# Hybrid decoder trunk on 8 cores: half-size filler pieces, a longer skew, masks added in PSUM, an early gate tile and another block order

## The chip, the cores and the metric

The kernel runs on all 8 cores of one Trainium2 chip. Each core computes 2 of the 16 sequences from end to end, with its own copy of the weights; the cores exchange nothing. A time is the device time of the slowest core in microseconds. A run of the kernel before took 4423.77 us in the median of 3 runs (3996.86 to 4560.96).

## The reference

Two layers, each a token mixer and a feed-forward part, on x of shape (16, 2048, 1024):

```
h = rms_norm(x) * g_pre;  proj = h @ w_in            # q, k, v of 16 heads, 2 gate logits of width 1024
o_A: dilated sliding window attention, 3 groups of 4 heads, (window, dilation) = (128,1), (512,4), (2048,16),
     the groups combined by their softmax denominators
o_B: 4 heads, causal block-sparse: own block of 256 keys + the best 3 past blocks (gate = q . mean(k of block))
y = (sigmoid(g_A) * (o_A @ W_A) + sigmoid(g_B) * (o_B @ W_B)) @ w_out;   x = x + rms_norm(y) * g_post
u = gelu(causal_dwconv3(h2 @ W_gate)) * (h2 @ W_up);                     x = x + rms_norm(u @ W_down) * g
```

Both attentions subtract m_h * (t - s) from the scores, and a query sees no later key.

## The kernel before, in words

Everything is written as Python generators. Each `yield c` says "about c us of TensorE work have been issued". `merge(main, fill, ratio)` (L83) steps the main generator and, for each c that it yields, lets the filler issue until it has yielded c * ratio. So the order of instructions on every engine is fixed when the program is built, and TensorE takes its own in that order: one that waits holds up all behind it. `par` interleaves generators by their yielded sums.

One sequence and one layer ("a layer" below; a core does four) goes through these stages:

1. Six dilated units (`dil_unit`, L660), 16 steps each, one step a tile of 128 keys for two heads. A step issues two score matmuls (L681) into a pair of PSUM banks, an exp on ScalarE (L689), a multiplication by the mask and distance factors on VectorE (L694), and, SKEW = 2 steps later, the products with V (`pv_mm`, L656) of the earlier tile. The filler is the projection work of the next unit: `v_proj` (L606) and `proj_fm` (L621), which issues 8 matmuls of 128x512 as one piece (`mm_group`, L383) and yields 1.75. The last unit, (2, 1), has two key and query projections of the block-sparse heads as filler; their evacuation puts a copy on ScalarE, a copy and for keys a reduction (L805) on VectorE. Every fourth step two banks of V products are copied by ScalarE (L372) and added into the accumulators by GpSimd (L740).
2. The block-sparse stage (`moba`, L868). It walks over 8 blocks (query group qg of 512, head pair); a block has 4 * qg + 4 key tiles times two heads, 160 units in all. A unit issues one score matmul (L935), an exp (L943), for the four diagonal key tiles a multiplication by the triangle on VectorE (L947), and 4 units later the V product (L656). When a block ends, VectorE copies the two accumulators (L964) and frees their banks (two banks only, so the next block's first V product needs that), and a chain of small transfers and VectorE operations follows that turns the denominators into factors: store, gather, reciprocal (L900), store, broadcast, multiply (L892). The steps of the chain are issued a fixed number of units after the end of the block (`todo`).
3. The filler of that stage (`fill_m`), ratio 1.25: the last projection, the block selection (`gating`, L809) of both pairs, the denominators of dilated pair 1 (`dil_den`, whose VectorE multiplications are L777), then it waits until the four blocks of query groups 0 and 1 are done, then `gates` (L975) for the first half of the tokens: per output chunk and token tile two gate projections of 8 matmuls, two tanh (L993, L999), two branch products of 2 matmuls (L383), and three VectorE operations (L1005, L1011, L1014). Each token tile of `gates` issues one of the 8 loads of `wout_t` once the last key tile of block (3, 0) has been issued, because that tile lies over the pair 0 operands.
4. `gates` for the second half, with `tail_out(0)` (output projection, L538, norms, residual) as filler; the first tanh there waits for the end of the block-sparse chains. Then the feed-forward part, L383 and L1242, whose first half has `tail_out(1)` as filler. The normalised tiles reach `hT` through transposing DMAs on SyncE's queue (L175).

The weights come through a ring of 8 slabs on GpSimd's queue (L180); each release waits on GpSimd for TensorE.

## Time and profile before

| | us |
|---|---|
| median of 3 runs (lowest, highest) | 4423.77 (3996.86, 4560.96) |
| profiled execution, its own time | 3906.2 |
| span of its slowest core (all: 3892.4 to 3904.9) | 3904.9 |
| TensorE busy | 3765.8 (96%) |
| VectorE, ScalarE, GpSimd busy | 2078.2, 1762.5, 877.7 |
| mean granted TensorE clock, by core | 0.991 to 0.994 |

Busy time of TensorE counts the tail of each matmul, so the 96% are a little kind. The trace's times below are microseconds from the start of the span of core 3. The first dilated unit of the first layer starts at 80.6, its last one at 243.1, the block-sparse stage at 269.1, and the 73rd of its 160 units at 320.6.

### The profile page before, as it was taken

The numbers are of one execution on the slowest core, as the hardware profiler recorded it, in microseconds if no ns is written. First come the engines' busy times: TensorE is split into PE (matmuls) and PEld (weight loads), VectorE is DVE, ScalarE is ACT, GpSimd is POOL, SyncE is SP. The second block draws the span as 40 slices with busy tenths as digits, with TensorE's granted clock in tenths as the row PEclk, the third lists the DMA queues.
The fourth block names the chain that finished last, engine by engine and source line by source line (L and its number), as shares of the span: only waits on it lengthen the run. The fifth ranks groups of instructions, "written<-read, shape, count | busy, mean of one in ns | idle before, by whom it ended". The sixth has DMA issues, their size and how long they took to land.

```text
span 3904.9 us, 56082 instructions; the slowest of 8 cores (3892.4 to 3904.9 us)
## 1 busy us (share of the span) xinstructions
PE 3765.8 (96%) x19760; PEld 1810.6 (46%) x19760; DVE 2078.2 (53%) x3265; ACT 1762.5 (45%) x3541; POOL 877.7 (22%) x1484
## 2 busy tenths in 40 slices
PE   6989999999998999999999899999999989999999
PEld 4544444444553444444465344444446534444444
DVE  4454566464346466646434646654643554675463
ACT  3456345253345635535334653552533465354251
POOL 2331232111132133211113213321111322331110
PEclk9999999999999999999999999999999999999999
DMA  6133789454313489875632259994442225797341
GB/s 147 29 72 51 153 173 169 112 97 90 81 32 65 60 165 177 149 171 79 129 79 53 48 77 167 158 156 124 77 105 52 53 47 92 161 179 133 103 71 70
DMA packets 303867, 410.37 MB, mean 105 GB/s; under 512 B 150560, under 2 KB 167200, under 8 KB 303584
## 3 DMA queue, kind: packets, MB, share of 16 engines
q0 software_dynamic: 118656, 190.89, 33.3%
q1 hardware_dynamic: 184944, 215.88, 21.6%
q8 instruction: 171, 2.80, 0.3%
q14 instruction: 96, 0.79, 0.1%
HBM read 500.52 MB, written 67.63 MB: 145 GB/s over the span
## 4 chain that ended last, share of the span: by engine, by line
PE 91%; DVE 4%; ACT 2%; DMA 1%; issue 1%; POOL 0%; SPq 0%; ACTq 0%; POOLq 0%; DVEq 0%
PE psum L383 55%; PE psum L1242 16%; PE psum L538 5%; PE psum L606 5%; PE psum L656 5%; PE psum L935 3%; PE psum L681 2%; ACT s_arena L943 1%; DMA s_xr<-x 1%; DVE s_arena L777 1%; DVE s_arena L694 1%; DVE s_arena L375 1%; ACT s_tz L372 0%; SPq L175 0%; DVE s_hb L460 0%
## 5 line engine op out<-in xcount | busy, mean ns | idle before, releaser
L383 PE MATMUL psum<-s_hT,s_slabs 128*128 128x512 bf16 x9728 | 2180.4, 380 | 12.3 <-DVE s_arena L1203 9.2
L383 PEld LDWEIGHTS psum<-s_hT,s_slabs 128*128 128x128 bf16 x9728 | 940.2, 98 | 1115.7 <-issue 32.1
L1242 PE MATMUL psum<-s_arena 128*128 128x512 bf16 x2816 | 609.1, 379 | 0.0
L1192 DVE SCALAR_TENSOR_TENSOR s_arena<-s_arena,s_convw 128x512 f32<-128x512 f32 x352 | 264.3, 751 | 425.9 <-ACT s_arena L1184 425.8
L1242 PEld LDWEIGHTS psum<-s_arena 128*128 128x128 bf16 x2816 | 275.6, 98 | 332.2
L656 PE MATMUL psum<-s_arena 128*128 128x128 bf16 (+2 forms) x1840 | 354.3, 268 | 63.7 <-DVE s_arena L947 21.5
L420 DVE SCALAR_TENSOR_TENSOR s_tz<-psum,s_stat,s_gpost 128x1024 f32<-128x1024 f32 x128 | 164.1, 1282 | 381.1 <-POOL s_stat L399 381.1
L411 ACT ACTIVATE s_hb<-psum 128x1024 bf16<-128x1024 f32 x128 | 131.0, 1023 | 502.2 <-PE psum L1242 344.0
L943 ACT ACTIVATE s_arena<-psum 128x512 bf16<-128x512 f32 (+3 forms) x640 | 296.1, 547 | 72.5 <-PE psum L935 61.1
L180 POOL DMA_DIRECT2D s_slabs<-w_in_r x224 | 122.5, 550 | 905.8 <-PE psum L656 453.6
L694 DVE TENSOR_TENSOR s_arena<-s_arena,s_dmask 128x512 bf16<-128x512 bf16 (+1 forms) x384 | 192.0, 504 | 217.9 <-ACT s_arena L689 216.2
L1183 ACT COPY s_arena<-psum 128x512 f32<-128x512 f32 x352 | 205.1, 583 | 203.7 <-PE psum L383 203.7
L396 POOL TENSOR_SCALAR s_stat<-s_stat 128x1 f32<-128x1 f32 x256 | 61.6, 241 | 1028.1 <-ACT s_hb L411 574.6
L689 ACT ACTIVATE s_arena<-psum 128x512 bf16<-128x512 f32 (+1 forms) x384 | 190.5, 504 | 200.0 <-PE psum L681 200.0
L1184 ACT ACTIVATE s_arena<-psum,s_convw 128x512 f32<-128x512 f32 x352 | 276.0, 784 | 0.0
L451 ACT ACTIVATE s_hb<-s_xr 128x1024 bf16<-128x1024 f32 x128 | 135.2, 1056 | 301.7 <-DVE s_xr L426 249.0
L1195 DVE SCALAR_TENSOR_TENSOR s_arena<-s_arena,s_convw 128x512 f32<-128x512 f32 x352 | 264.7, 752 | 12.5
L180 POOL DMA_DIRECT2D s_slabs<-w_gate_r x176 | 97.5, 554 | 749.6 <-PE psum L383 747.7
L460 DVE SCALAR_TENSOR_TENSOR s_hb<-s_xr,s_stat,s_gpre 128x1024 bf16<-128x1024 f32 x128 | 164.3, 1284 | 175.9 <-POOL s_stat L399 167.6
L606 PE MATMUL psum<-s_slabs,s_hT 128*128 128x256 bf16 x2048 | 250.1, 275 | 5.1 <-DVE s_arena L375 5.1
L1203 DVE TENSOR_TENSOR s_arena<-s_arena,psum 128x512 bf16<-128x512 f32 x352 | 239.5, 680 | 3.6 <-ACT s_arena L1201 3.6
L935 PE MATMUL psum<-s_arena 128*128 128x512 bf16 (+3 forms) x640 | 225.2, 361 | 8.5 <-ACT s_arena L943 5.7
(71 smaller groups left out, 3278.9 us busy)
## 6 DMA issues: line engine op xcount, KB each, us to landing
s_slabs<-w_in_r POOLq DMA_DIRECT2D x224, 256.0 KB, 4.8
xs<-s_xr SPq DMA_DIRECT2D x96, 512.0 KB, 3.9
s_xr<-xs SPq DMA_DIRECT2D x96, 512.0 KB, 5.2
s_slabs<-w_gate_r POOLq DMA_DIRECT2D x176, 256.0 KB, 4.6
s_slabs<-w_up_r POOLq DMA_DIRECT2D x176, 256.0 KB, 5.7
s_xr<-x SPq DMA_DIRECT2D x64, 512.0 KB, 6.4
s_arena<-w_down POOLq DMA_DIRECT2D x88, 256.0 KB, 7.3
y<-s_xr SPq DMA_DIRECT2D x32, 512.0 KB, 2.9
```

The costliest lines, as they stand in the source:

```text
L180: q.eng.dma_start(out=out, in_=in_, **kw).then_inc(so.sem, 16)
L383: inst = nc.tensor.matmul(out, lhsT=l_, rhs=r_, start=(i == 0), stop=(i == n - 1))
L606: inst = nc.tensor.matmul(ps[b][:, 0:256], lhsT=hT[:, kc, start:start + 127 * d + 1:d], rhs=rhs, start=(kc == 0), stop=(kc == 7))
L656: return nc.tensor.matmul(out, lhsT=V[:, tile, VOFF[hd]:VOFF[hd] + 128], rhs=rhs, start=start, stop=stop)
L694: ptoks[kt] = DVE.do(nc.vector.tensor_tensor(out=Pd[sl][:, :, 0:nq], in0=Pd[sl][:, :, 0:nq], in1=dmask[:, head:head + 2, 0:nq], op=ALU.mult))
L935: tS = PE.do(nc.tensor.matmul(ps[bS][:, 0:nq], lhsT=Kx[:, kt * 128:(kt + 1) * 128], rhs=Qx[:, qg * 512 + c0:(qg + 1) * 512], start=True, s ...
L943: tE = ACT.do(nc.scalar.activation(out=Pm[sl][:, 0:nq], in_=ps[bS][:, 0:nq], func=AF.Exp))
L1184: tt1 = ACT.do(nc.scalar.activation(out=t1_, in_=ps[b_a], func=AF.Identity, bias=convw[:, l, fc, 3:4], scale=convw[:, l, fc, 2:3]))
L1192: d1 = DVE.do(nc.vector.scalar_tensor_tensor(out=t1_, in0=a_[:, 1 + 512 * tgi:513 + 512 * tgi], scalar=convw[:, l, fc, 1:2], in1=t1_, op0= ...
L1195: d2 = DVE.do(nc.vector.scalar_tensor_tensor(out=t1_, in0=a_[:, 512 * tgi:512 + 512 * tgi], scalar=convw[:, l, fc, 0:1], in1=t1_, op0=ALU. ...
L1203: u1 = DVE.do(nc.vector.tensor_tensor(out=uT[:, u["fc"], u["tsl"]], in0=u["t1"], in1=ps[u["b_u"]], op=ALU.mult))
L1242: inst = nc.tensor.matmul(ps[zb + n], lhsT=uT[:, kc, i * 128:(i + 1) * 128], rhs=wdn[kc][:, n * 512:(n + 1) * 512], start=(kc == 0), stop= ...
```

## The change

- `merge` takes any number of fillers, each with its own ratio. `scaled` multiplies what a generator yields, `pause` yields without issuing.
- `proj_fm` and the gate projections yield after 4 of 8 matmuls (0.87) and after the other 4 (0.87).
- The skew in `dil_unit` is 3, not 2.
- In `moba`, the diagonal tiles of query groups 0 and 1 get their mask from a second matmul, identity times `ntri` (128 columns), accumulated on the scores before the exp; the VectorE multiplication remains for groups 2 and 3. The exp waits for the last dilated V product (`p_free`) and no longer for GpSimd's accumulation.
- The blocks run (2,0), (3,0), (2,1), (3,1), before (2,0), (2,1), (3,0), (3,1).
- In the norm chain of the first four blocks the gather is issued after 5 units (6), the reciprocal after 11 (16), the multiplication after 17 (16).
- The filler of the block-sparse stage becomes two fillers of ratio 1.25: `side` (selection of both pairs, the second after a pause of 8, and the denominators) and `fill_pe` (the last projection stretched by 1.5, then `gates`). `gates` issues the gate projections and tanh of output chunk 0 early, stretched by 3.4, into buffers of their own (`AB0`), then waits for `ready()`, then continues.

```diff
@@ def proj_fm
-                tp = mm_group(ps[b], [(buf[:, kc * 128:(kc + 1) * 128], hT[:, kc, tg * 512:(tg + 1) * 512]) for kc in range(8)],
-                              [tokw, hT_tok[4 * tg:4 * tg + 4]])
+                for kc in range(8):
+                    inst = nc.tensor.matmul(ps[b], lhsT=buf[:, kc * 128:(kc + 1) * 128], rhs=hT[:, kc, tg * 512:(tg + 1) * 512],
+                                            start=(kc == 0), stop=(kc == 7))
+                    if kc == 3:
+                        yield 0.87
+                tp = PE.do(inst)
                 bank_free[b] = consume(tg, b, tp)
-                yield 1.75
+                yield 0.87
@@ def dil_unit
-            SKEW = 2
+            SKEW = 3
@@ def moba
-            blocks = [(0, 0), (1, 0), (0, 1), (1, 1), (2, 0), (2, 1), (3, 0), (3, 1)]
+            blocks = [(0, 0), (1, 0), (0, 1), (1, 1), (2, 0), (3, 0), (2, 1), (3, 1)]
-                todo.append([16 if k < 4 else 28, lambda: norm_mult(k, qg, pair, rt)])
+                todo.append([17 if k < 4 else 28, lambda: norm_mult(k, qg, pair, rt)])
-                todo.append([6 if k < 4 else 10, gather])
-                todo.append([16 if k < 4 else 24, lambda: norm_recip(k, qg, pair, tl)])
+                todo.append([5 if k < 4 else 10, gather])
+                todo.append([11 if k < 4 else 24, lambda: norm_recip(k, qg, pair, tl)])
+                    diag = kt >= 4 * qg
+                    pe_mask = diag and qg < 2
+                    inst = nc.tensor.matmul(ps[bS][:, 0:nq], lhsT=Kx[:, kt * 128:(kt + 1) * 128],
+                                            rhs=Qx[:, qg * 512 + c0:(qg + 1) * 512], start=True, stop=not pe_mask)
+                    if pe_mask:
+                        inst = nc.tensor.matmul(ps[bS][:, 0:128], lhsT=identb[:, :], rhs=ntri[:, :], start=False, stop=True)
-                    ACT.wait(tS, pfree[sl], waits)
+                    ACT.wait(tS, pfree[sl], p_free)
-                    if kt >= 4 * qg:
+                    if diag and not pe_mask:
@@ def gates (each token tile: gate_mm = 2 x 8 matmuls and tanh, branch_mm = 2 x 2 matmuls and the VectorE part)
+            if early is not None:
+                bufs, e_wait, factor, ready = early
+                for tgi in range(2):
+                    yield from scaled(gate_mm(0, tgi, bufs, e_wait), factor)
+                while not ready():
+                    yield 0.5
+                for tgi in range(2):
+                    yield from branch_mm(0, tgi, bufs)
+                first = 1
@@ def mixer
-            def fill_m():
-                yield from par(chain(mqk_proj(l, 1, 0, w1, mq[1], FB2), gating(1, mq[1], aug_t[1], sel[1], FB2)),
-                               gating(0, mq[0], aug_t[0], sel[0], FB2), dil_den(1, m_wait, nt1))
-                while not all((q, p) in done for q in range(2) for p in range(2)):
-                    yield 0.5
-                yield from gates(l, 0, nt1, ob_done, FB2, nt1, mts, wout_load)
-            merge(moba(mq, aug_t, sel, vt[3], done, m_wait, on_p0), fill_m(), 1.25)
+            def ready():
+                return len(nt1) == 4 and all((q, p) in done for q in range(2) for p in range(2))
+            def fill_pe():
+                yield from scaled(mqk_proj(l, 1, 0, w1, mq[1], FB2), 1.5)
+                yield from gates(l, 0, nt1, ob_done, FB2, nt1, mts, wout_load, (AB0, nt0, 3.4, ready))
+            side = par(chain(pause(8.0), gating(1, mq[1], aug_t[1], sel[1], FB2)),
+                       gating(0, mq[0], aug_t[0], sel[0], FB2), dil_den(1, m_wait, nt1))
+            merge(moba(mq, aug_t, sel, vt[3], done, ures[(2, 1)]["pv_tok"], m_wait, on_p0), (side, 1.25), (fill_pe(), 1.25))
```

## Rows read from the trace of the kernel before

**Rows 1.** The page: busy time of the engines; chain that ended last, by engine.
```profile
PE 3765.8 (96%) x19760; PEld 1810.6 (46%) x19760; DVE 2078.2 (53%) x3265; ACT 1762.5 (45%) x3541; POOL 877.7 (22%) x1484
...
PE 91%; DVE 4%; ACT 2%; DMA 1%; issue 1%; POOL 0%; SPq 0%; ACTq 0%; POOLq 0%; DVEq 0%
```
**Rows 2.** Windows: stretch, length, busy by engine (x count), clock, DMA share, GB/s.
```profile
80.60:117.40 36.80, 36.48 (x288) 24.05 (x288) 14.66 (x32) 15.67 (x31) 3.95 (x6) 1.00 0.34 49
...
211.40:243.10 31.70, 29.23 (x187) 13.16 (x186) 19.90 (x33) 15.80 (x32) 13.23 (x13) 1.00 0.49 86
243.10:269.10 26.00, 20.43 (x128) 8.93 (x126) 15.85 (x28) 13.09 (x33) 13.32 (x10) 1.00 0.32 59
...
305.60:320.60 15.00, 13.02 (x49) 4.86 (x48) 6.83 (x20) 11.38 (x24) 0.00 (x0) 0.77 0.12 37
...
512.00:704.00 192.00, 191.90 (x889) 86.72 (x888) 127.41 (x165) 104.10 (x217) 52.48 (x106) 1.00 0.88 169
```
**Rows 3.** Chain that ended last, one feed-forward piece: start, us, what.
```profile
609.45 94.97 PE psum L383 x440
```
**Rows 4.** Timeline of TensorE in the last dilated unit: start, us, what [idle before].
```profile
258.04 0.22 PE L656 MATMUL psum<-s_arena 128*128 128x128 bf16 x1 [1.07 <-DVE s_km L805]
...
258.48 1.89 PE L383 MATMUL psum<-s_hT,s_slabs 128*128 128x512 bf16 x8
...
264.47 0.22 PE L656 MATMUL psum<-s_arena 128*128 128x128 bf16 x1 [1.07 <-DVE s_km L805]
...
268.59 0.27 PE L656 MATMUL psum<-s_arena 128*128 128x128 bf16 x2 [1.31 <-DVE s_arena L694]
```
**Rows 5.** Timeline of VectorE there.
```profile
257.19 0.69 DVE L805 TENSOR_REDUCE s_km<-psum 128x2 f32<-128x512 f32 x1
...
257.80 0.28 DVE L694 TENSOR_TENSOR s_arena<-s_arena,s_dmask 128x256 bf16<-128x256 bf16 x1
```
**Rows 6.** TensorE by shape, 269.1 to 320.6: busy us, mean ns, idle before.
```profile
L935 PE MATMUL psum<-s_arena 128*128 128x512 bf16 x42 | 17.2, 427 | 0.6 <-ACT s_arena L943 0.3 <-issue 0.3
L656 PE MATMUL psum<-s_arena 128*128 128x512 bf16 x42 | 16.8, 403 | 4.2 <-DVE s_arena L947 1.4 <-DVE s_gsm L840 1.1 <-DVE s_cdm L900 1.0
L383 PE MATMUL psum<-s_hT,s_slabs 128*128 128x512 bf16 x32 | 7.6, 379 | 0.7 <-ACT s_tz L372 0.7
...
L858 PE MATMUL psum<-s_identb,s_gsel 128*8 128x128 bf16 x32 | 2.4, 219 | 0.0
```
**Rows 7.** Waits of TensorE, 269.1 to 320.6: us in total, times, longest.
```profile
PE psum L656 <- DVE s_arena L947: 5.5, 5, 1.4
PE psum L935 <- ACT s_arena L943: 1.3, 2, 0.9
PE psum L656 <- DVE s_gsm L840: 1.1, 2, 0.8
```
**Rows 8.** ScalarE's exp and VectorE's mask, 269.1 to 320.6.
```profile
L943 ACT ACTIVATE s_arena<-psum 128x512 bf16<-128x512 f32 (+3 forms) x72 | 31.7, 524 | 13.4 <-PE psum L935 10.6 <-POOL s_xr L740 2.7
...
L947 DVE TENSOR_TENSOR s_arena<-s_arena,s_tri 128x128 bf16<-128x128 bf16 x39 | 7.8, 220 | 13.8 <-ACT s_arena L943 13.4
```
**Rows 9.** Timeline, end of the block-sparse stage: TensorE, SyncE's queue, VectorE, ScalarE.
```profile
400.54 0.22 PE L656 MATMUL psum<-s_arena 128*128 128x128 bf16 x1
...
413.21 0.35 SPq L180 DMA_DIRECT2D dm<-s_cdm  x1
418.71 1.08 SPq L180 DMA_DIRECT2D s_arena<-dm  x2
...
428.95 1.40 DVE L892 TENSOR_TENSOR s_arena<-s_arena 64x512 bf16<-64x512 f32 x2
...
430.38 0.60 ACT L993 ACTIVATE s_arena<-psum 128x512 f32<-128x512 f32 x1 [3.19 <-DVE s_arena L892]
```
**Rows 10.** Timeline, feed-forward start of the third layer: SyncE's queue, TensorE.
```profile
2504.19 12.19 SPq L175 DMA_TRANSPOSE s_hT<-s_hb  x1
...
2547.67 2.72 PE L383 MATMUL psum<-s_hT,s_slabs 128*128 128x512 bf16 x6 [8.91 <-DVE s_arena L1203]
```

More of the change, by code:

```diff
@@ L80, with merge, scaled, pause @@
 KB = 256
-def merge(main, fill, ratio):
-    credit = 0.0
-    live = fill is not None
+def merge(main, *fills):
+    live = [[gen, ratio, 0.0] for gen, ratio in fills]
     for cost in main:
-        credit += cost * ratio
-        while live and credit > 0:
-            try:
-                credit -= next(fill)
-            except StopIteration:
-                live = False
-    if live:
-        for _ in fill:
-            pass
+        for f in list(live):
+            f[2] += cost * f[1]
+            while f[2] > 0:
+                try:
+                    f[2] -= next(f[0])
+                except StopIteration:
+                    live.remove(f)
+                    break
+    for f in live:
+        for _ in f[0]:
+            pass
+def scaled(gen, factor):
+    for cost in gen:
+        yield cost * factor
+def pause(cost):
+    for _ in range(int(2 * cost)):
+        yield 0.5
 def chain(*gens):
@@ L572, in build @@
         AB = [carve((12 + 2 * i) * KB, 512) for i in range(4)]
+        AB0 = [carve((60 + 2 * i) * KB, 512) for i in range(4)]
         uT = carve(0, 11264, BF16).rearrange("p (c t) -> p c t", c=NFC)
@@ new lines, in gates, with gate_mm @@
+            w = {}
+            def gate_mm(oc, tgi, bufs, waits):
+                tg = 2 * hf + tgi
+                tsl = slice(tg * 512, (tg + 1) * 512)
+                if tgi == 0:
+                    w[oc] = [load_w(l, 24 + oc), load_w(l, 32 + oc)]
+                out = []
+                for j in range(2):
+                    buf, tok, s_ = w[oc][j]
+                    b = banks.get()
+                    PE.wait(tok, hT_tok[4 * tg:4 * tg + 4])
+                    inst = None
+                    for kc in range(8):
+                        inst = nc.tensor.matmul(ps[b], lhsT=buf[:, kc * 128:(kc + 1) * 128], rhs=hT[:, kc, tsl], start=(kc == 0), stop=(kc == 7))
+                        if kc == 3:
+                            yield 0.87
+                    t_g = PE.do(inst)
+                    ACT.wait(t_g, abf[2 * tgi + j], waits)
+                    s1 = ACT.do(nc.scalar.activation(out=bufs[2 * tgi + j], in_=ps[b], func=AF.Tanh, scale=0.5))
+                    bank_free[b] = [s1]
+                    out.append(s1)
+                    if tgi == 1:
+                        slab_ring.release(s_, t_g)
+                    yield 0.87
+                w[(oc, tgi)] = out
@@ L1286, in qk_tg @@
                     next(gen)
+                    next(gen)
                 yield
```

93 lines of the change are left out of this document (41 added, 52 removed).

## The prediction

> **What bounds the kernel now.** I read the page first: TensorE is busy for 96% of the span and the chain of work that ended last lies on it for 91% [rows 1]. So only what shortens TensorE's own queue, or the holes in it, can move the end. The windows by stage show where the holes are: the feed-forward stretch has 0.1 us of idle time in 192, the first dilated unit 0.3 in 36.8, but the fifth unit 2.5 in 31.7, the last one 5.6 in 26.0, and the first 72 units of the block-sparse stage have long waits and, in their last 15 us, a granted clock of 0.77 [rows 2]. The rest of the layer is paid in matmuls at full rate: 440 of 128x512 in 94.97 us, 0.216 us each [rows 3]. I use that as the price of 512 columns, and a quarter of it, 0.054, for 128.
>
> How much is to be had: in the block-sparse stretch from 269.1 to 320.6 (51.5 us) TensorE has 42 + 42 + 32 matmuls of 512 columns, 25.1 us, and the smaller shapes and the selection come to some 8.7 us more by their columns: 33.8 us of work, so 17.7 us are lost [rows 6]. Waits for another engine explain some 10, of which the group of waits has the three largest [rows 7]. The slow clock explains about 3.5: 15.0 us at 0.77 are 6.9 us at 1.2 GHz, half of it lost [rows 2]. The rest is scores and V products short of exps. With the 8.1 us of the two last dilated units that makes about 26 us a layer, 103 in all, 2.6%: hardly more is to be had here.
>
> The sum is made against the profiled execution, 3906.2 us (span 3904.9). The median of the runs shown is 4423.77, 13% above it, and none of the three came down to it (lowest 3996.86). I carry the saving over as a ratio.
>
> **The last dilated unit.** Once in four steps (6.4 us) the V product waits 1.07 us, put down to VectorE's key reduction, and the filler of 8 matmuls, 1.89 us, comes only behind it [rows 4]. VectorE began the reduction at 257.19 for 0.69 us and the mask product at 257.80 [rows 5]: the product that TensorE needed stood behind it. Skew 3 puts one step more between the exp and the V product, 0.22 us of matmuls and, with pieces of half size, 0.87 us of filler in every step instead of 1.73 in every second. That is 1.1 us more, about one such wait. I take 3.7 of the unit's 5.6 us away; bounds 1.5 (where the wait just moves to the copies that free the V banks, 0.3 us each four steps) and 5. At the end of each unit the V product of tile 15 waits for its mask, 1.31 us at the last one [rows 4]; one more V product of 0.2 us stands before it, so 0.2 a unit, 1.2 for six, bounds 0 and 2. The fifth unit's idle time I leave, but for that. Sum 4.9, rounded down to 4.5 because splitting pieces also lets the bank of a projection be held longer.
>
> **The masks in PSUM.** 32 diagonal units a layer lose their VectorE product (0.22 us and a semaphore hop [rows 8]) and gain a matmul of 128 columns. 5.5 us of TensorE waits ended with that product, 5 times [rows 7]; only the one in block (2, 0) keeps it. I take away 4.4. The price is 32 x 0.054 = 1.7 us, above it 32 x 0.075 = 2.4 by the busy time of the 32 selection transposes of 128 columns, 2.4 us [rows 6]. I take 1.7, as these stand between other matmuls.
> For the same price the Trainium skill ("TensorE: Matmul & The Clock Gate", Back-to-back issue gap) states about 81 ns for each weight load and matmul of 128 columns in a stream; by it the masks would cost 2.6 us a layer, 10.4 in all, where I have 7, and the saving would be 46 us. No row here shows 81; the transposes, tails included, have 75.
>
> **The exp's wait.** The first exp stood 2.7 us behind GpSimd's accumulation [rows 8]; it now goes when the last V product is done. TensorE had 1.3 us of waits for exps and most of its 0.7 us at the first filler piece in that place [rows 6, 7]; I take 1.5 us.
>
> **The early gate tile.** Four groups of 8, 32 x 0.216 = 6.9 us of TensorE work, are issued between units 20 and 63 (10.4 of stretched projection, then 7 x 3.4 = 23.8, at 0.54 a unit). Moved work saves nothing by itself; it saves what it puts into holes. ScalarE has 31.7 us of exps in 51.5 us [rows 8], plus 4 tanh of 0.6: it doesn't bind. The holes left there after the two edits above are 17.7 - 4.4 - 1.5 = 11.8 us, 3.5 of it slow clock. With fewer and shorter stops I expect the clock to stay up (3) and one more microsecond filled. What is late next: the V banks behind VectorE's copies at each block's end, and these behind the selection's operations (1.1 us [rows 7]) and the denominator products. So about 7.8 remain. Check: 33.8 + 1.7 + 6.9 + 7.8 = 50.2 us to the 73rd unit instead of 51.5, with 6.9 us of gate work done: 8.2 us a layer. Bounds: 4 (only the mask and exp waits go, and the clock doesn't rise) and 13.
>
> **What costs nothing.** One constant load of 32 KB at the start. The earlier reciprocal can stop VectorE for its gather, but with no mask behind it no exp product waits. `ready()` is true at about unit 78, before 82: the same gates earlier, hidden in a stretch already full. The order of the blocks moves 8 loads of the output weights 24 units forward; they land long before the first output tile, before as after.
>
> **The end of the stage.** The filler is used up earlier. Gates take 70.4 of yields at 0.54 a unit, before from unit 83 to 214; now 63.4 from 78 to 196, so TensorE gets about 16 us of filler behind the last V product instead of the 26.7 seen from 400.54 [rows 9]. The chain of the last block: reciprocal's store at +12.7, its landing 5.5 us later, broadcast, multiplication at +28.4, only then the first tanh, which had waited 3.19 us [rows 9]. The multiplication comes behind the last filler piece on VectorE and so moves up to about +24. Behind the filler TensorE has four gate groups, two branch pairs and one output tile, 6.9 + 1.7 + 3.5 = 12 us, that need no tanh: cover to +28. So no hole, but thin cover: 0.3 us as cost, bounds 0 and 4.
>
> **Sum.** 4.5 + 8.2 - 0.3 = 12.4 us a layer, 50 in four: 3856 us for the profiled execution, 1.3% less. On the median that is 4423.77 x 0.987 = 4367.
>
> **Rivals.**
> *More (chance 0.12).* All early stops go, and the 15 us at a clock of 0.77, which came after mask waits of up to 1.4 us [rows 2, 7], with them. Then 13 + 7 = 20 us a layer, 80 us, 3826 (median 4333), over 2% faster. Against it: TensorE takes its queue in order, and the V bank waits are untouched.
> *Less (0.22).* The holes are latencies in series (score, exp, product, V bank) and the filler stands in front of the waits without shortening them; masks cost 1.7. Then 1.5 + 3 = 4.5 a layer, 18 us, 3888 (4404). For it: TensorE was idle although filler of 7 us lay in the first 13 units.
> *The change does not get to its place (0.06)*: half pieces and skew 3 cancel out (the third step without scores at each unit's end is not covered): 0 +- 8 us, 3906.
> *Slower (0.06).* The transposing DMAs ahead of the feed-forward part. In the third layer one occupied SyncE's queue for 12.19 us and TensorE stood 8.91 us with the clock down after it [rows 10], 13 us in all against the other layers. Earlier weights could bring such a pile-up to every layer and to both tails: 2 x 13 x 4 = 104 against 50 gained, 3960 (4485), 1.4% slower. It decides from 6 us of stall a tail. Against it: DMA share is 0.88 there already [rows 2] without a stall, and the output weights leave that place earlier.
>
> **Numbers.** A measurement of this kernel tells 2% from no change. My forecast has 0.54; over 2% faster 0.12, within 2% 0.84 (forecast, less, no effect and the milder part of slower), over 2% slower 0.04 (stalls half as long again). In the profiled execution's terms 8 in 10 lie between 3830 and 3915. The runs shown spread by 14%, far more than any case here, and the time after is one of that kind; so the range goes from the low end of the first, 3835, to the highest run shown with little gained, 4560.96 x 0.998 = 4550.
>
> **What would show it.** Right: the last dilated unit at 21 to 23.5 us for 26.0; no mask wait of TensorE in the first 48 block-sparse units; the 73rd unit at about 50 us from the first, with 32 gate matmuls before it, no stretch there under 0.9 of clock; gaps behind the last block under 1 us; feed-forward windows unchanged. Wrong: the same waits with VectorE's copies as releaser, or a first tanh of the second half behind L892 for over 8 us with TensorE idle.

## The result and the profile after

The changed kernel takes 3859.1 us, the median of its runs, and the kernel before some 3904 us beside it: a ratio of 0.989, 95% interval 0.986 to 0.992. The change makes it faster by 1.1%, more than the comparison is uncertain and less than 2%. In some runs of either kernel the cores of one die are slowed and the time is up to 18% longer; all the runs of before that the prediction was shown (3996.86 to 4560.96) were of this kind, while the profiled execution of 3906.2 us and the times compared below are not. The profiled execution after took 3857.86 us, 48.3 us less than the one before; its slowest core took 3856.3 us from first to last instruction.

The page after, lines as in [rows 1], and the group of V products:

```profile
span 3856.3 us, 56276 instructions; the slowest of 8 cores (3849.7 to 3856.3 us)
...
PE 3763.9 (98%) x19888; PEld 1816.3 (47%) x19888; DVE 2062.1 (53%) x3137; ACT 1773.1 (46%) x3541; POOL 876.4 (23%) x1484
...
PE 93%; DVE 3%; ACT 2%; issue 1%; DMA 0%; POOL 0%; SPq 0%; ACTq 0%; DVEq 0%; POOLq 0%
...
L676 PE MATMUL psum<-s_arena 128*128 128x128 bf16 (+2 forms) x1840 | 351.9, 265 | 27.1 <-DVE s_kmb L840 9.0
```

TensorE is busy for as long as before, 3763.9 us for 3765.8, though it has 128 matmuls more; only its idle time shrank, from 139 us to 92. The windows after, in the order of [rows 2] (first, fifth and sixth dilated unit, the first block of the block-sparse stage, its next three, the fifth up to the 73rd unit, a feed-forward stretch):

```profile
83.30:119.80 36.50, 36.45 (x286) 23.97 (x286) 14.55 (x32) 15.57 (x31) 3.87 (x6) 1.00 0.33 50
215.00:245.20 30.20, 29.37 (x185) 12.94 (x184) 20.31 (x32) 15.77 (x31) 11.34 (x12) 1.00 0.48 88
245.20:270.00 24.80, 21.34 (x131) 8.73 (x129) 19.83 (x31) 13.60 (x34) 14.48 (x12) 0.99 0.32 65
270.00:279.70 9.70, 9.16 (x52) 4.22 (x53) 1.05 (x3) 4.58 (x11) 3.01 (x2) 0.67 0.21 30
279.70:308.90 29.20, 27.57 (x193) 14.29 (x192) 19.52 (x65) 20.12 (x45) 0.57 (x1) 1.00 0.29 66
308.90:321.50 12.60, 12.44 (x59) 4.77 (x56) 5.84 (x16) 11.79 (x27) 3.17 (x6) 1.00 0.55 85
500.00:692.00 192.00, 191.89 (x889) 86.70 (x888) 129.02 (x167) 102.64 (x211) 53.34 (x109) 1.00 0.88 165
```

The last dilated unit still has 3.5 us without work for TensorE (before 5.6). On this core and in this layer the slow clock that lay in the last 15 us up to the 73rd unit is gone from there and stands at the beginning of the stage. Over all cores and layers there is less of it: the time at the lower clock is 57.8 us a core before and 36.7 after. Ahead of the first dilated unit and in the rest of the layers it hardly changed (together 24.5 and 22.2 us), but in the last dilated unit and the block-sparse stage it fell from 33.3 to 14.5 us, from 8.3 to 3.6 us a layer. At half the speed, half of such time is lost, so this gives back 2.4 us a layer. The feed-forward part is what it was.

One core of one execution is a thin base for terms of a microsecond. For the comparisons below every trace is split at the first score matmul of each dilated unit, of the block-sparse stage and of its 73rd unit, and at the stage's last score. The columns are means over the four layers; "rest" goes from the last block-sparse score to the next layer's first dilated score, "layer" from one layer's first dilated score to the next layer's, both as the mean of the first three layers. Cores whose trace lacks records of block-sparse scores are left out of all columns but those two, which leaves six (three in the lines marked *):

```
us                        dilated units 1 to 6           sum    first 72  stage   rest   layer
before                    36.9 37.0 27.5 29.7 31.4 26.7  189.2  51.5      130.0   640.5  959.5
changed kernel            36.7 36.6 28.4 30.6 30.4 24.9  187.5  50.1      128.6   633.0  948.6
 skew 2                   36.9 37.0 27.5 29.4 30.0 23.6  184.4  49.9      128.7   633.3  946.1
 skew 4                   36.5 36.3 28.7 29.8 29.3 23.2  183.9  49.3      127.8   632.9  944.4
 whole filler pieces      36.7 36.6 27.9 30.2 31.0 26.4  188.7  51.6      133.1   632.5  953.8
 accumulation left out    36.7 36.3 28.2 30.6 30.4 22.6  184.7  48.6      127.1   633.0  944.6
 accumulation on VectorE  36.7 39.8 32.6 30.7 35.5 27.6  202.8  50.5      129.0   632.9  964.1
 skew 2, four-piece add * 36.9 36.5 26.9 29.4 29.7 25.8  185.2  49.6      128.1   632.8  945.8
 masks on VectorE         as the changed kernel          187.5  51.9      130.4   632.7  949.9
 no early gate tile       as the changed kernel          187.6  47.6      125.5   640.3  952.9
 exp's wait as before     as the changed kernel          187.6  50.7      129.2   633.0  949.5
 old order of the blocks  as the changed kernel          187.5  50.2      128.8   633.2  949.0
before, with skew 3 *     36.7 36.6 28.2 29.8 31.1 23.6  186.0  52.1      130.6   640.3  957.0
```

By this table the change takes 1.7 us off the dilated part, 1.4 off the block-sparse stage and 7.5 off the rest, and 10.9 us off a layer from start to start, 44 in four. The third layer's transposing DMAs, which cost the profiled core of before 13 us [rows 10], have no long one after, and TensorE waits there for 3.0 us:

```profile
2508.39 51.92 PE L396 MATMUL psum<-s_hT,s_slabs 128*128 128x512 bf16 x232 [2.97 <-DVE s_arena L1250]
```

That layer's rest is 5.6 us longer than the mean of the two before it, on this core as on the others; before, it was 12.5 us longer on the profiled core and 3.6 to 5.3 on the other seven. So the profiled core of before carried some 7 us that the others did not, and the pair of profiled executions flatters the change by that much. The change did not remove the stall of a typical core.

In the block-sparse stage the waits on masks are gone. TensorE's waits from 270.0 to 321.5 after, beside [rows 7], and its groups there, beside [rows 6]:

```profile
PE psum L676 <- DVE s_arena L989: 0.6, 1, 0.6
PE psum L643 <- ACT s_tz L385: 0.5, 1, 0.5
PE psum L676 <- DVE s_gsm L860: 0.5, 1, 0.5
PE psum L957 <- ACT s_arena L968: 0.3, 1, 0.3
```
```profile
L1017 PE MATMUL psum<-s_hT,s_slabs 128*128 128x512 bf16 x32 | 8.2, 379 | 0.0
L960 PE MATMUL psum<-s_ntri,s_identb 128*128 128x128 bf16 x32 | 7.5, 233 | 0.0
```

The 32 mask matmuls and the 32 gate matmuls are where the prediction placed them. Over the complete cores and all layers TensorE has 2.2 us without work between the stage's start and the 73rd unit; before it had 9.9. At the end of the stage stands one wait of 1.0 us, before the first output tile. The multiplication came at 425.98, some 24 us behind the last V product (402.1), as the prediction had it:

```profile
421.83 3.61 PE L551 MATMUL psum<-s_arena 128*128 128x512 bf16 x16 [1.01 <-DVE s_arena L1048]
...
425.98 1.40 DVE L912 TENSOR_TENSOR s_arena<-s_arena 64x512 bf16<-64x512 f32 x2 [4.41 <-DMA s_arena<-dm]
```

What is left at the seam between the dilated part and the block-sparse stage is this. TensorE, VectorE and GpSimd at the end of the last dilated unit, changed kernel:

```profile
266.73 0.66 PE L676 MATMUL psum<-s_arena 128*128 128x128 bf16 x5 [0.15 <-ACT s_tz L385]
269.56 0.37 PE L676 MATMUL psum<-s_arena 128*128 128x128 bf16 x2 [2.17 <-DVE s_kmb L840]
...
267.15 0.69 DVE L825 TENSOR_REDUCE s_km<-psum 128x2 f32<-128x512 f32 x1 [0.17 <-ACT s_arena L385]
267.76 1.65 DVE L714 TENSOR_TENSOR s_arena<-s_arena,s_dmask 128x256 bf16<-128x256 bf16 x1
269.33 0.16 DVE L840 TENSOR_SCALAR s_kmb<-s_km 128x8 bf16<-128x8 f32 x1
...
266.24 3.02 POOL L760 TENSOR_TENSOR s_xr<-s_xr,s_tz 128x512 f32<-128x512 f32 x2 [2.34 <-ACT s_tz L385]
```

The V product of the last tile needs the mask product that began at 267.76. Such a product takes 0.28 us elsewhere [rows 5]; here it took 1.65 and ended at 269.41, just behind GpSimd's two additions (269.26). The wait is put down to L840 only because that was VectorE's last instruction. Behind the 2.17 us of idle time the granted clock falls here: the first 52 matmuls of the stage took 9.7 us at a mean of 0.67. Between the levels of 2.4 and 1.2 GHz that is two thirds of the stretch at the lower one. In the second layer the clock stayed up, and 52 matmuls took 6.2 us:

```profile
1220.00:1226.20 6.20, 6.20 (x52) 3.42 (x53) 1.05 (x3) 4.48 (x11) 3.02 (x2) 1.00 0.36 48
```

The wait is there in every layer, 2.2 to 2.3 us, so it does not decide alone. In the 24 seams of the six complete cores the clock fell around the stage's first score in 22; with skew 2 and a wait of 1.38 us in 19, with the accumulation left out and 0.8 to 0.9 us in 2. Yet before, with 1.31 us there and 1.08 us four microseconds earlier, it fell in 8 only. What else decides stays open.

### The profile page after: what moved, and what is told of

Read it like the earlier page. It is cut to its first block, busy times and chain, and to the rows that moved or that the text cites. A ratio compares the mean times of both kernels' runs of the same rounds, so it can differ in the third digit from the quotient of the medians.

```text
span 3856.3 us, 56276 instructions; the slowest of 8 cores (3849.7 to 3856.3 us)
## 1 busy us (share of the span) xinstructions
PE 3763.9 (98%) x19888; PEld 1816.3 (47%) x19888; DVE 2062.1 (53%) x3137; ACT 1773.1 (46%) x3541; POOL 876.4 (23%) x1484
## 4 chain that ended last, share of the span: by engine, by line
PE 93%; DVE 3%; ACT 2%; issue 1%; DMA 0%; POOL 0%; SPq 0%; ACTq 0%; DVEq 0%; POOLq 0%
PE psum L396 34%; PE psum L1289 16%; PE psum L1017 11%; PE psum L643 11%; PE psum L551 6%; PE psum L676 5%; PE psum L620 5%; PE psum L957 3%; PE psum L701 2%; ACT s_tz L385 1%; DVE s_arena L714 1%; DVE s_hb L473 0%; DMA s_xr<-x 0%; ACT s_arena L385 0%; ACT s_hb L464 0%
## 5 line engine op out<-in xcount | busy, mean ns | idle before, releaser
L396 PE MATMUL psum<-s_hT,s_slabs 128*128 128x512 bf16 x5632 | 1224.0, 379 | 3.0 <-DVE s_arena L1250 3.0
L643 PE MATMUL psum<-s_hT,s_slabs 128*128 128x512 bf16 x2048 | 497.7, 382 | 4.8 <-DVE s_arena L389 3.1
L1017 PE MATMUL psum<-s_hT,s_slabs 128*128 128x512 bf16 x2048 | 489.6, 379 | 0.4
L968 ACT ACTIVATE s_arena<-psum 128x512 bf16<-128x512 f32 (+3 forms) x640 | 306.0, 539 | 90.8 <-PE psum L957 63.5
L1242 DVE SCALAR_TENSOR_TENSOR s_arena<-s_arena,s_convw 128x512 f32<-128x512 f32 x352 | 264.7, 752 | 12.5
```

Source lines behind the costliest of these rows:

```text
L396: inst = nc.tensor.matmul(out, lhsT=l_, rhs=r_, start=(i == 0), stop=(i == n - 1))
L643: inst = nc.tensor.matmul(ps[b], lhsT=buf[:, kc * 128:(kc + 1) * 128], rhs=hT[:, kc, tg * 512:(tg + 1) * 512], start=(kc == 0), stop=(kc = ...
L968: tE = ACT.do(nc.scalar.activation(out=Pm[sl][:, 0:nq], in_=ps[bS][:, 0:nq], func=AF.Exp))
L1017: inst = nc.tensor.matmul(ps[b], lhsT=buf[:, kc * 128:(kc + 1) * 128], rhs=hT[:, kc, tsl], start=(kc == 0), stop=(kc == 7))
L1242: d2 = DVE.do(nc.vector.scalar_tensor_tensor(out=t1_, in0=a_[:, 512 * tgi:512 + 512 * tgi], scalar=convw[:, l, fc, 0:1], in1=t1_, op0=ALU. ...
```

## Experiments

The first four ask what the dilated part lost, since 1.7 us a layer are there instead of 4.5.

**Skew 2 in the changed kernel.**
```
-            SKEW = 3
+            SKEW = 2
```


> The changed kernel with the skew of the dilated units back at 2; all else as changed. Lengths are counted from the first score matmul of a unit to that of the next. Changed kernel: last unit 24.8 to 25.0 us, all six units 187.5 in the mean of four layers; before: 26.2 (28.1 once) and 189.3. Theory of the prediction (the V product waits behind VectorE, and one more step covers it): the last unit goes back to 26 or more, all six to 189.5. Rival (what holds the V product is longer than a step, so the skew hardly matters, and only the half pieces gave the 1.3 us): last unit 25.2 or less, all six within 1 us of 187.5.

Measured: 3848.1 us (3843.9 and 3852.3), ratio to before 0.985 (0.980 to 0.990), 11 us less than the changed kernel. The longer skew, which the prediction counted as the gain, is a loss beside half pieces: the sum of the units falls from 187.5 to 184.4 when it is taken back. Neither the theory nor the rival had that.

**Whole filler pieces in the changed kernel.** The groups of eight matmuls, in the projections and in the gate tiles, are again issued without a yield in between (the cut of `proj_fm`; that of the gate projections is the same):
```
-                    if kc == 3:
-                        yield 0.87
-                yield 0.87
+                yield 1.74
```


> The changed kernel with filler pieces of 8 matmuls again, in the projections and the gate tiles. The third and fourth unit had become longer with the change (27.5 to 28.4 and 29.7 to 30.6 us), with a gap of 0.33 us every four steps at the V product that needs a bank back from ScalarE's copy. Theory A (half pieces leave only 0.87 us of filler before each such V product, where a whole piece covered the copy): third and fourth unit return to 27.4 and 29.8, the last unit rises to about 26. Theory B (the skew does it): both stay at 28.4 and 30.6. Block-sparse stage: first 72 units up by 1 to 3 us from 50 if half pieces matter there, unchanged if not.

Measured: 3879.2 us (3877.0 to 3879.9), ratio 0.993 (0.991 to 0.995). Taken out of the changed kernel, half pieces are worth 20 us, 5.2 us a layer, and most of it not where the prediction had looked: 1.2 us in the dilated units, 4.5 in the block-sparse stage, of which 1.5 up to the 73rd unit and 3.0 behind it. Those 3.0 are not a gain on the kernel before, which with its whole pieces takes 78.5 us from the 73rd unit to the last score, as the changed kernel does: whole pieces cost there only together with the other edits.

**The accumulation all but left out.** GpSimd's addition of the partial V sums runs over one column of 512, so that part of the sum is missing:
```
-    te = POOL.do(nc.gpsimd.tensor_tensor(out=dst, in0=dst, in1=src, op=ALU.add))
+    te = POOL.do(nc.gpsimd.tensor_tensor(out=U[:, m:m + 1], in0=U[:, m:m + 1],
+                                         in1=ust[k][:, 0:1], op=ALU.add))
```


> The changed kernel with GpSimd's accumulation of the dilated groups 2 and 3 cut to one column (the addition is left out; ScalarE's copies remain). In the trace mask products of VectorE that overlap one of GpSimd's additions take 1.0 us in the median and up to 3.14, the others 0.29 (128x256). Theory L (VectorE's product with two inputs in SBUF is held until GpSimd's addition ends, and that holds the V product): all mask products at 0.29 or 0.43, last unit 24.9 to 21.5, stall of 2.2 us before the block-sparse stage under 1 and no half clock after it, all six units 187.5 to 182. Theory B (the banks that ScalarE's copies free are the limit): mask products shorter, but the last unit stays above 24.3 and the 0.33 us gaps remain.

Measured: 3842.2 us, 17 less than the changed kernel. VectorE and TensorE at the same place:

```profile
268.74 0.28 DVE L714 TENSOR_TENSOR s_arena<-s_arena,s_dmask 128x256 bf16<-128x256 bf16 x1
...
269.17 0.27 PE L676 MATMUL psum<-s_arena 128*128 128x128 bf16 x2 [0.80 <-DVE s_kmb L840]
```

The product is back at 0.28 us and the wait at 0.80. Over the whole trace of the changed kernel the 100 products of 128x256 that met no addition had a median of 0.29 us, the 68 that met one 1.00, up to 3.14. With the short additions all of that is gone, the last unit falls from 24.9 to 22.6 us and the first 72 block-sparse units by 1.5. So GpSimd's additions, which no step of the prediction priced, cost 4 us a layer. The time at the lower clock falls with them from 36.7 to 24.2 us a core; half of the difference, 1.6 us a layer, is part of the 4. That VectorE is the way is shown by its products; what the additions cost otherwise, as by GpSimd's own queue, was not separated.

**The accumulation on VectorE**, straight from PSUM, without ScalarE's copy:
```
-    tc_ = copy_on(ACT, ust[k], ps[ub])
-    te = POOL.do(nc.gpsimd.tensor_tensor(out=dst, in0=dst, in1=src, op=ALU.add))
+    te = DVE.do(nc.vector.tensor_tensor(out=dst, in0=dst, in1=ps[ub], op=ALU.add))
+    bank_free[ub] = [te]
```


> The changed kernel with the accumulation moved: VectorE adds straight from PSUM into the accumulator, ScalarE's copy and GpSimd's addition are gone (same results). VectorE gets 8 operations of about 0.68 us a unit in four of six units, ScalarE loses 8 of 0.59, GpSimd 8 of 1.55. Theory L (hold behind GpSimd): as with the addition left out, less what VectorE's own time costs: last unit 22 to 23 us, all six 183 to 185, with the clock 4 x 6 = 24 us less than the changed kernel, ratio to before 0.982. Rival (VectorE becomes the bound: in the last unit 15.9 + 5.4 of 24.9 us busy, and the masks queue behind the additions): last unit 25 to 27, no gain, 0.989 or worse.

Measured: 3927.5 us, 68 more than the changed kernel, worse than even the rival expected. What takes the hold away puts the V banks behind VectorE's queue. TensorE's waits, whole trace:

```profile
PE psum L676 <- DVE s_xr L755: 39.0, 48, 1.4
...
PE psum L676 <- DVE s_arena L755: 27.4, 38, 1.0
```

Next, what skew 3 loses to skew 2. A theory by the phase of the filler, that is, by which steps of a unit have filler in front of their V product: when the V product that opens a new pair of banks falls into a step with little filler, ScalarE's two copies of the banks (1.07 us) or VectorE's products show.

**Skew 4 in the changed kernel**, run twice:
```
-            SKEW = 3
+            SKEW = 4
```


> The changed kernel with skew 4. With skew 3 the third to fifth unit have steps with one and with two half pieces in turn, and the V product that fills a bank falls in a step with one; with skew 2 it fell in one with two. Theory P (parity: ScalarE's two copies of 1.07 us are hidden only behind two half pieces): skew 4 behaves as skew 2 there, fourth unit 29.4 us (skew 3: 30.6), third 27.1 to 28.0 (28.1 to 28.7). Rival (a longer skew costs by itself, since a unit starts with that many steps without V products and ends with as many without scores or filler): fourth unit 31 or more, third 29. Last unit by both: no shorter than with skew 3 by more than 1 us, as the hold behind GpSimd stays.

> The changed kernel with SKEW = 4 in the dilated units instead of 3, the version I would keep, timed again because its first profile had a stretched die. My theory (with skew 3 the V product that opens a new bank falls into a step that has a single half piece of filler; with 2 or 4 into a step with two) expects 3838 to 3846 us, below the changed kernel by 13 to 21, fourth unit 29.8 and last unit 23.3 us in every undisturbed core. The rival, that each step of skew only costs the length of one more empty step at a unit's end, expects more than 3859, about 3862.

Measured: the first time four runs took 4010.0 to 4527.7 us, and only the spans of cores 4 to 7 of the profiled one compare, 3833.7 to 3837.6 us; the second time 3845.0 us median (three runs at 3843.6 to 3846.0, one at 3860.0), ratio to before 0.986 (0.983 to 0.989). Not more skew costs, but 3: fourth unit 29.7 us before, 30.6 with 3, 29.8 with 4, 29.4 with 2. The wait at the end of the last unit is another now:

```profile
266.11 0.22 PE L676 MATMUL psum<-s_arena 128*128 128x128 bf16 x1 [1.24 <-DVE s_km L825]
...
265.86 0.28 DVE L714 TENSOR_TENSOR s_arena<-s_arena,s_dmask 128x256 bf16<-128x256 bf16 x1
266.06 1.50 DVE L840 TENSOR_SCALAR s_kmb<-s_km 128x8 bf16<-128x8 f32 x1
...
266.00 3.02 POOL L760 TENSOR_TENSOR s_xr<-s_xr,s_tz 128x512 f32<-128x512 f32 x2 [2.48 <-ACT s_tz L385]
```

The mask product slipped in ahead of the additions, and the one held is a small key operation that TensorE does not need at once. Skew 4 and skew 2 are equal within their runs, and either beats both kernels. The third unit goes against the theory: it takes 28.7 us with skew 4, as long as with 3 (28.4) and not as with 2 (27.5).

**Skew 3 alone on the kernel before**, with its whole pieces:
```
-            SKEW = 2
+            SKEW = 3
```


> The kernel before with SKEW = 3 alone, whole filler pieces kept. The prediction held that skew takes the wait of 1.07 us that returned every four steps of the last unit; as the pieces stand behind the V product in every second step, it would be worth 1.5 to 3 us a layer: 3890 to 3896, last unit 24 to 25 us for 26.5. By the parity theory a gain at the last unit is paid back at units 3 to 5, where the bank-filling V product changes from the step with a filler piece to the one without: 3900 to 3912, fourth unit over 30.2 us for 29.7.

Measured: 3892.0 us for the lowest run, 10 to 14 less than before (3901.5 to 3905.9 beside it), 2.5 us a layer by the table, the last unit at 23.6 us for 26.7. The prediction's value for this unit, 3.7 us, holds about here (3.1), and my rule of payback at units 3 to 5, which asked for a fourth unit over 30.2 us, does not (29.8). What differs is seen when this trace is laid beside the one with whole pieces in the changed kernel: both have skew 3 and whole pieces in the last unit. The unit takes 25.4 us there and 22.4 here at full clock, 27.0 and 23.9 where the clock falls within it, so three microseconds either way. The last unit, in the changed kernel with whole pieces (first and second layer) and in the kernel before with skew 3 (second layer of one core, first layer of another):

```profile
243.80:269.20 25.40, 20.70 (x130) 9.15 (x130) 16.48 (x29) 13.18 (x33) 11.99 (x9) 1.00 0.32 64
1197.50:1224.50 27.00, 22.33 (x131) 9.39 (x128) 15.92 (x29) 13.11 (x33) 11.90 (x9) 0.94 0.30 59
```
```profile
1201.70:1225.60 23.90, 21.65 (x131) 9.20 (x129) 16.92 (x28) 13.12 (x33) 13.23 (x10) 0.93 0.34 67
242.20:264.60 22.40, 20.13 (x131) 8.96 (x129) 17.35 (x28) 13.16 (x33) 13.27 (x10) 1.00 0.38 72
```

TensorE's waits in the last unit, first the changed kernel with whole pieces (first layer; the second has the same), then the kernel before with skew 3 (second layer):

```profile
PE psum L674 <- DVE s_km L823: 2.2, 2, 1.1
PE psum L674 <- ACT s_tz L385: 1.5, 3, 1.2
PE psum L674 <- DVE s_arena L712: 0.8, 1, 0.8
```
```profile
PE psum L656 <- DVE s_arena L694: 2.1, 2, 1.4
```

And the place of the filler around the V product that opens new banks, in the same order:

```profile
252.57 0.28 PE L674 MATMUL psum<-s_arena 128*128 128x128 bf16 x2
252.78 0.23 PE L699 MATMUL psum<-s_arena 64*128 64x128 bf16 x2
254.18 0.50 PE L674 MATMUL psum<-s_arena 128*128 128x128 bf16 x2 [1.16 <-ACT s_tz L385]
254.59 1.89 PE L643 MATMUL psum<-s_hT,s_slabs 128*128 128x512 bf16 x8
```
```profile
1215.16 0.23 PE L681 MATMUL psum<-s_arena 64*128 64x128 bf16 x2
1215.32 0.28 PE L656 MATMUL psum<-s_arena 128*128 128x128 bf16 x2
1215.45 1.89 PE L383 MATMUL psum<-s_hT,s_slabs 128*128 128x512 bf16 x8
1217.27 0.23 PE L681 MATMUL psum<-s_arena 64*128 64x128 bf16 x2
1217.43 0.29 PE L656 MATMUL psum<-s_arena 128*128 128x128 bf16 x2
```

Counted from the unit's first score, the opening products are those of the steps 3, 7, 11 and 15. In the first kernel such a step (252.78) follows the V product before it at once, its piece comes only behind its own V product (254.59), and TensorE stands for 1.16 us; the next two such steps stand for 1.07 and 1.08. In the second a piece of 1.89 us lies ahead of each such step (1217.27), and no wait is left until the end of the unit. The kernel before has waits of the first kind, 1.07 us each [rows 4]. One more step of skew removed them there. Half pieces leave no step bare, and beside skew 3 they removed the waits of 1.07 to 1.16 us (in the changed kernel those places wait 0.16); then the second of the two has nothing to remove. That the place of the filler is the cause is read from two traces of kernels that differ in more than it; half pieces alone in the kernel before were not run.

**GpSimd's addition in four pieces**, with skew 2:
```
-    te = POOL.do(nc.gpsimd.tensor_tensor(out=dst, in0=dst, in1=src, op=ALU.add))
+    for p_ in range(4):    # a_, b_: a quarter of the columns of dst and src each
+        te = POOL.do(nc.gpsimd.tensor_tensor(out=a_, in0=a_, in1=b_, op=ALU.add))
```


> The changed kernel with skew 2 and GpSimd's accumulation in four instructions of 128 columns for each one of 512. With skew 2 alone: 3848 us, last unit 23.6 us, stall of 1.5 us at its end, mask products in its shadow up to 1.65 us. Theory L (a mask product is held until GpSimd's running instruction ends): the hold is at most one short instruction, 0.4 to 0.5 us; last unit 22 to 22.8, end stall about 1, 2 to 3 us a layer with the clock, so 3836 to 3842. Rival (GpSimd's next piece gets in again before VectorE, or its fixed cost makes the four much longer than one): mask products stay at 1 us or more, accumulation over 2.5 us a tile instead of 1.55, last unit 23.6 or longer, 3848 or more.

Measured: 3852.8 us the lowest run, profiled execution 3875.7 us, last unit 25.8 us for 23.6: no gain over skew 2, as the rival had it. Eight short additions back to back held one product 3.43 us, about as long as two long ones can (3.14 in the changed kernel):

```profile
243.86 3.43 DVE L714 TENSOR_TENSOR s_arena<-s_arena,s_dmask 128x256 bf16<-128x256 bf16 x1 [0.45 <-ACT s_arena L709]
...
243.34 3.81 POOL L765 TENSOR_TENSOR s_xr<-s_xr,s_tz 128x128 f32<-128x128 f32 x8
```

The last four take block-sparse edits one by one out of the changed kernel. The shifted steps of the norm chain, the stretching of the projection and the split of the filler in two were not taken out alone.

**Masks on VectorE again.**
```
-                    pe_mask = diag and qg < 2
+                    pe_mask = False
```


> The changed kernel with the masks of all diagonal tiles on VectorE again (no mask matmul). Theory of the prediction: the masks in PSUM take away 4.4 us of waits a layer for 1.7 of matmuls, so the first 72 block-sparse units get 2.7 us longer (changed kernel: 51.4, 48.0, 49.6, 51.2 us, of which up to 3.4 is slow clock), 11 us in all, 3869. Rival (the half pieces and the early gate tile cover those waits anyway): the stretch gets 1 to 2 us shorter by the matmuls left out, 3850 to 3854 in all.

Measured: 3867.3 us, 8 more; the first 72 units take 51.9 us instead of 50.1, and a layer 1.3 us more. So the masks in PSUM are worth 1.3 to 2 us a layer. TensorE waits there for the mask products 1.3 us a layer, where it waited 5.4 before the change, and for all engines 4.8 instead of 2.2: the expectations' rival is right in that the other edits had covered most of those waits, and wrong in that it expected a gain from leaving the masks out.

**No early gate tile.** The early argument is gone, and the gates begin, as before, when the blocks are done:
```
-    ... gates(..., wout_load, (AB0, nt0, 3.4, ready))
+    while not ready():
+        yield 0.5
+    ... gates(..., wout_load)
```


> The changed kernel without the early gate tile: the filler of TensorE waits for ready() after the projection and then does all of gates. Theory of the prediction: the tile's 6.9 us mostly go into holes, so that the first 72 units get only 3 to 4 us shorter without it and a layer 3 to 4 us longer, 12 to 16 us in all (3870 to 3874). Rival (the holes are waits in TensorE's own order, which the tile stands in front of): the 72 units get 6 to 7 us shorter and the whole stays within 4 us of 3858. A clock fall in the emptier stretch would add 1.7 us a time on top.

Measured: 3879.8 us, 21 more, 4.3 a layer by the table. The stage then takes 125.5 us instead of 128.6, and the rest of the layer 640.3 instead of 633.0: the tile's 6.9 us of work cost 3.1 where they were put and saved 7.3 where they had been. Two things pay for it. Up to the 73rd unit TensorE is without work for 5.3 us without the tile and 2.2 with it. And without it a core spends 12.8 us of its four layers at the lower clock between 15 us after the stage's start and the 73rd unit, with it none; half of that is 1.6 us a layer.

**The exp's wait as before**, for everything of the dilated part:
```
-    merge(moba(..., ures[(2, 1)]["pv_tok"], m_wait, on_p0), ...
+    merge(moba(..., m_wait, m_wait, on_p0), ...
```


> The changed kernel with the first exps of the block-sparse stage waiting as before, for everything of the dilated part and so for GpSimd's last addition, instead of the last V product. The prediction gave this wait 1.5 us a layer: 3865. If it is hidden because the scores of the first units wait for the matmuls and the slow clock anyway, 3859 within 2, with the first block (0, 0) at 7.9 us as in the changed kernel. If the exps that start earlier only ask for the same slots, the time may even fall by 1 to 2 us.

Measured: 3864.1 us for the lower run, 5 more; a layer takes 0.9 us more in the mean, 0.3 to 0.6 by medians. The first block (0, 0) takes 9.0 us for 8.3, so the wait is not hidden. Some 1 us a layer, less than the 1.5 of the prediction, on one run.

**The blocks in the old order.**
```
-            blocks = [..., (2, 0), (3, 0), (2, 1), (3, 1)]
+            blocks = [..., (2, 0), (2, 1), (3, 0), (3, 1)]
```


> The changed kernel with the blocks of the block-sparse stage in the old order, (2, 0), (2, 1), (3, 0), (3, 1). The prediction gave the order no price: 3859 within 2, the rest of the layer unchanged at 631.9 us. The rival is that the output weights, which go out only behind the last score of pair 0, come 24 units later and delay either the end of the stage or the transposing DMAs before the feed-forward part: rest of a layer 1 to 3 us longer, 3863 to 3870, or the third layer's stall back from about 6 to 13 us, 3866.

Measured: 3860.3 us (3859.3 and 3861.2), the rest of the layer 633.2 for 633.0. The order that loads the output weights sooner is worth nothing, as predicted.

## Why the prediction was wrong in its number

**The step that failed is the carrying over.** "I carry the saving over as a ratio" put 50 us of the profiled execution onto the median of the runs shown, and gave 4367. The same section says that the profiled execution took 3906.2 us and that no run shown came down to it; that was the evidence that these runs were lengthened by something that is not in the trace, and a kernel's time without it is the profiled one. It went on to say of the spread runs that "the time after is one of that kind"; it was not: the median after is 3859.1. The sum against the profiled execution, 3856, stands 2 us from the profiled execution after (3857.9) and 3 from the median. Some of that is luck: 50 us were forecast, and a typical core saves 44; the profiled execution of before held some 7 us of a stall that its other cores did not have. The wide range (3835 to 4550) held the result only because it was stretched over both. Of the chances, "within 2%" (0.84) is where the result lies; but 1.1% with an interval of 0.8 to 1.4 is told apart from no change, so 2% was too coarse a statement of what a measurement of this kernel can tell.

**The sum came out near by terms that were off on both sides**, which is luck again: too much in the dilated part, too little in the rest.

- *Dilated part: 4.5 us a layer forecast, 1.7 measured.* "Skew 3 puts one step more between the exp and the V product" was priced at 3.7 us of the last unit, together with half pieces. Skew alone in the kernel before brings the unit from 26.7 to 23.6 us, and the changed kernel with skew 2, so with half pieces alone, has 23.6 too. Together they gave 24.9, where the last mask product falls under GpSimd's additions (2.17 us of wait against 0.80 without them), and the third and fourth units grew by 0.9 us each. The unit's gain of 1.8 us is near the bound of 1.5 that the prediction named, "where the wait just moves to the copies that free the V banks", but what it moved to was not these copies.
- *End of each unit: 1.2 forecast.* The first two units gained 0.2 and 0.4, not all of it at their ends; at the last one the wait grew from 1.31 [rows 4] to 2.17 us.
- *Masks in PSUM: 4.4 - 1.7 = 2.7 us forecast, 1.3 to 2 measured.* No wait on a mask is left in the first 48 units, so the 4.4 are had, but most of them go to the other edits as well: with the masks back on VectorE only 1.3 us of such waits return, and 2.7 of all waits. The price of the matmuls, 1.7, was not too low. Start to start a mask matmul takes 0.05 to 0.06 us among its neighbours at full clock, as the prediction's 0.054, and not the 81 ns that it quotes from the Trainium skill:

```profile
278.09 0.22 PE L957 MATMUL psum<-s_arena 128*128 128x128 bf16 x1
278.14 0.22 PE L960 MATMUL psum<-s_ntri,s_identb 128*128 128x128 bf16 x1
278.20 0.33 PE L676 MATMUL psum<-s_arena 128*128 128x384 bf16 x1
```

- *The exp's wait: 1.5 forecast, about 1 measured*, from one run.
- *Masks, exp, tile and clock together, up to the end of the stage and the rest: 8.2 us forecast, 8.9 measured* (1.4 in the stage and 7.5 in the rest). The 73rd unit came at 50.1 us, forecast 50.2, and here the mechanism was right: the forecast took 6.9 us of idle time (4.4, 1.5 and 1) and 3 us of slow clock out of the 17.7 lost, and measured are 7.7 (9.9 to 2.2) and, with the last dilated unit, 2.4. The tile alone is worth 4.3 us.
- *Half pieces in the block-sparse stage: not in the sum, 4.5 us when they are taken out.* The prediction weighed the splitting in one dilated unit only and even rounded down for it. But 3.0 of the 4.5 are a loss that the kernel before did not have, so the term missing from a sum that starts there is at most 1.5. Why the other edits need short pieces was not looked into.
- *"I expect the clock to stay up (3)": right in the stage, not at its seam.* The slow stretch ahead of the 73rd unit [rows 2], 6.3 us a layer on all cores and layers, is gone everywhere. At the seam it grew from 2.0 to 3.6 us a layer, and in the profiled core's first layer to the 9.7 us for what takes 6.2 at full clock. Half of the difference is 2.4 us a layer, of 3 forecast. The prediction's sign "no stretch there under 0.9 of clock" did not hold.
- *End of the stage: 0.3 a layer forecast, 1.0 seen, before the first output tile.* The cover was as thin as was said, and enough.
- *Order of the blocks: nothing forecast, nothing measured.*

Masks, tile, exp's wait, order and half pieces, each taken out alone, are worth 1.3, 4.3, 0.9, 0.4 and 5.2 us a layer by the table; less the 2.5 that skew 3 costs, that is 9.6 of the 10.9 found. The edits lean on each other (masks and tile, half pieces and the rest), so that they add up this well is no proof of each.

Of the rivals, "less" had the right reason for the dilated part, and "slower" did not come: the rest of no layer got longer. What stays open is why the third layer stalls at all, why the clock falls at the seam in most layers and not in all, and what shifts the filler's phase against the V banks from one unit to the next; these differ between kernels that have the same order of work there.

## What to carry to other kernels

A wait that returns every few steps in a merged stream is a matter of phase: look at which step has no filler, and try a step of skew and a finer filler each alone before both, since each may remove all there is. Taking an edit out of the finished kernel prices it beside the others, not against the kernel before. If the runs shown all lie far above the profiled execution, predict the time from the profiled one. And before pricing a queue, list which of its instructions got longer beside another engine's (here VectorE's mask products beside GpSimd's additions), and where these will overlap after the shift.

## What the runs showed of the hardware

VectorE's product of two SBUF operands and GpSimd's addition do not run side by side: 0.28 us alone, 1.00 in the median when it met an addition, up to 3.14 under two of 1.5 us each (3.55 with skew 4), 3.43 under eight short ones in a row, and where it is held it ends some 0.15 us behind the additions (269.41 and 269.26, 247.29 and 247.15 above). Held products had nearly always begun during an addition: of 18 that began before one, on one core each of the traces with skew 4 and with four pieces, 16 kept 0.28 us. The Trainium skill ("SBUF — State Buffer", Who interferes with whom) states that a VectorE instruction with two SBUF inputs contends with a GpSimd instruction that reads SBUF, and that the later one is blocked until the other is done; the trace agrees, and adds that it can stay blocked over several GpSimd instructions that follow one another. A VectorE operation on 128x8 elements with a single SBUF input was held too, 1.50 us for 0.16. The reductions and casts with PSUM inputs kept their 0.69 us beside such additions. The chain of waits shows none of this as GpSimd's: the sign is one operation of one shape with two durations.
